# Small fills dealt evenly among the projection pieces, and conversions queued behind the last mixer's own work

## What is computed

```python
h = rms_norm(x, g1) @ W_in                        # columns split among A, B, C, D
qa, ka, va, qb, kb, vb, qc, kc, vc, qd, kd, vd = split(h)
oa = stick_breaking(qa, cache+ka, cache+va)        # scan over keys
oc = rms_norm((softmax(s0) - lam * softmax(s1)) @ vc)   # two halves per head
od = softmax(band(qd @ kd) + rel_bias) @ vd
ob = softmax_with_sink(window(qb @ kb) + t5_bias) @ vb
x = x + concat(oa, ob, oc, od) @ W_out
x = x + (silu(rms_norm(x) @ W_gate) * (rms_norm(x) @ W_up)) @ W_down
```

## Time and profile before

| | us |
|---|---|
| median of 3 runs | 1555.75 (1548.22 to 1557.88) |
| the profiled execution's own time | 1557.51 |
| its span | 1555.7 |
| rounds of A, C, D, B in the span | about 91 to 238, 238 to 444, 444 to 603, 603 to 700 |
| granted clock of TensorE, mean | 0.973 of full speed |

### The profile page before, as it was taken

One profiled execution on the slowest core, in us unless ns is written; L12 is line 12 of the kernel. 1 busy time (PEld: TensorE's weight loads), 2 busy tenths in 40 slices (PEclk: granted clock), 3 DMA queues, 4 the chain that ended last, 5 costly groups with the idle time before them and its releaser, 6 DMA issues.

```text
span 1555.7 us, 23204 instructions
## 1 busy us (share of the span) xinstructions
PE 1482.5 (95%) x8997; PEld 1307.6 (84%) x8997; DVE 691.8 (44%) x1259; ACT 417.0 (27%) x1030; POOL 270.5 (17%) x428
## 2 busy tenths in 40 slices
PE   5999999899999987999999999999999999999997
PEld 3987788687787776668899999989898999999896
DVE  6326564556533233544534444342525344443516
ACT  5123345445445545652310000101010100001013
POOL 7115454433331101122400000000000000000002
PEclk8999999799899998999999999999999999999999
DMA  7211002100011013111121111101101011110003
GB/s 210 68 62 51 15 27 66 48 15 15 15 55 47 16 32 132 42 28 41 57 80 55 41 41 54 54 27 54 54 27 54 27 54 40 42 53 27 0 0 128
DMA packets 90481, 75.93 MB, mean 49 GB/s; under 512 B 5671, under 2 KB 83016, under 8 KB 90396
## 3 DMA queue, kind: packets, MB, share of 16 engines
q1 hardware_dynamic: 90412, 75.00, 15.8%
HBM read 64.06 MB, written 10.77 MB: 48 GB/s over the span
## 4 chain that ended last, share of the span: by engine, by line
PE 87%; DVE 4%; ACT 4%; POOL 2%; issue 1%; DMA 1%; SPq 0%; ACTq 0%; DVEq 0%; POOLq 0%
PE acc L739 25%; PE acc L741 24%; PE acc L740 24%; PE acc L881 5%; PE acc L905 3%; PE acc L943 2%; PE acc L927 2%; POOL xlo L1572 1%; DVE acc L1360 1%; DVE low_z L1357 1%; PE acc L754 1%; PE acc L1049 1%; DVE wo_lo L1415 1%; DVE olo L1410 0%; PE acc L805 0%
## 5 line engine op out<-in xcount | busy, mean ns | idle before, releaser
L739 PE MATMUL acc<-ohi,gu_hi 128*128 128x384 f32 (+1 forms) x1056 | 344.3, 326 | 1.8 <-issue 1.8
L741 PE MATMUL acc<-ohi,gu_lo 128*128 128x384 f32 (+1 forms) x1056 | 344.2, 326 | 0.0
L740 PE MATMUL acc<-olo,gu_hi 128*128 128x384 f32 (+1 forms) x1056 | 344.0, 326 | 0.0
L1237 ACT ACTIVATE silu<-acc 128x384 f32<-128x384 f32 (+1 forms) x66 | 31.2, 473 | 638.6 <-PE acc L741 638.6
L739 PEld LDWEIGHTS acc<-ohi,gu_hi 128*128 128x128 f32 x1056 | 198.2, 188 | 2.7 <-issue 2.2
L740 PEld LDWEIGHTS acc<-olo,gu_hi 128*128 128x128 f32 x1056 | 198.2, 188 | 0.4
L741 PEld LDWEIGHTS acc<-ohi,gu_lo 128*128 128x128 f32 x1056 | 198.2, 188 | 0.0
L1493 DVE TENSOR_TENSOR prod<-acc,silu 128x384 f32<-128x384 f32 (+1 forms) x66 | 35.4, 536 | 336.7 <-ACT silu L1237 336.7
L1513 DVE TENSOR_TENSOR x<-acc,x 128x512 f32<-128x512 f32 x198 | 134.5, 689 | 69.1 <-PE acc L741 64.4
L1563 POOL TENSOR_SCALAR meansq<-sumsq 128x1 f32<-128x1 f32 (+1 forms) x27 | 9.2, 342 | 803.7 <-ACT sq_junk L1077 769.1
L741 PE MATMUL acc<-dn_hi,h_lo 128*128 128x512 f32 x352 | 137.1, 389 | 0.0
(11 more groups left out here) (202 smaller groups left out, 2512.1 us busy)
## 6 DMA issues: line engine op xcount, KB each, us to landing
win_raw<-in_w_in_dram SPq DMA_DIRECT2D x22, 512.0 KB, 3.9
gu_raw<-in_w_gate_dram SPq DMA_DIRECT2D x22, 512.0 KB, 3.9
gu_raw<-in_w_up_dram SPq DMA_DIRECT2D x22, 512.0 KB, 4.8
down_raw<-in_w_down_dram SPq DMA_DIRECT2D x22, 512.0 KB, 3.8
x_in<-in_x_prompt_dram SPq DMA_DIRECT2D x8, 512.0 KB, 7.0
wo_raw<-in_w_out_dram SPq DMA_DIRECT2D x8, 512.0 KB, 3.5
x<-in_x_prompt_dram SPq DMA_DIRECT2D x8, 512.0 KB, 5.2
out_dram<-y_out SPq DMA_DIRECT2D x8, 512.0 KB, 2.6
```

Source lines behind the costliest of these rows:

```text
L739: pe.matmul(out, a_hi, b_hi, start=first, stop=False)
L740: pe.matmul(out, a_hi, b_lo, start=False, stop=False)
L741: return pe.matmul(out, a_lo, b_hi, start=False, stop=last)
L1237: act.activation(silu[:, q % 2, 0:n], bank(2 * (q % 2), n), ACT.Silu).then_inc(silu_done, 1)
```

## The change

Two parts. **(1)** `mixed` loses its `every` and deals the small fills evenly over the whole list of big ones; and the cache fills, and the last rows fills of C and D, are dealt among the projection pieces of the next mixer and no longer stand as a run between the values and the projections. By the planner's own arithmetic on the new lists, no work is added or taken away (106 fills in both); what a round holds changes, in the planner's cost units (about microseconds of TensorE):

| rounds | before | after |
|---|---|---|
| 2 to 7 (A) | 6.2, 4.8, 1.4, 6.2, 0.5, 0.5 | 3.4, 6.2, 3.4, 6.2, 4.7, 4.2 |
| 8 to 15 (A) | 8.8, 7.7, 5.1, 5.6, 4.2, 2.1, 6.5, 4.2 | 5.6, 2.1, 6.4, 3.8, 2.1, 6.8, 3.8, 2.1 |
| 30 to 34 (C) | 0.5, 0.5, 4.7, 0, 4.2 | 0.5, 2.1, 2.1, 2.1, 2.1 |
| 44 to 46 (C) | 4.2, 0.9, 3.5 | 2.1, 2.7, 1.8 |
| 59 to 62 (D) | 1.4, 0.5, 8.8, 3.5 | 3.5, 4.2, 2.1, 6.1 |
| 63 to 71 (D) | 7.1, 5.6, 5.1, 7.7, 3.2, 3.7, 3.7, 2.1, 3.2 | 2.1, 8.2, 9.2, 6.0, 3.2, 3.7, 2.1, 3.2, 2.1 |

Rounds 18 to 29 and 54 to 58 keep what they had, and B's rounds have no fills. In round 69 both halves of the value fill at place 1 are gone; a rows fill at place 0 and a value fill at place 2 remain. The last pieces that use W_in slabs 19, 20 and 21, from which the rounds of W_out's conversions are counted, stay in rounds 64, 66 and 71.

**(2)** Each conversion keeps its round, and moves from the head of the round to its end: in ScalarE's queue behind `normalize`, in VectorE's behind everything but the adds of the output projection. A wait for the fourth `olo` goes before a memset in round 74.

```diff
-    def mixed(big, small, every):
-
-        small = list(small)
+    def mixed(big, small):
+
+        big, small = list(big), list(small)
+        done = 0
         for k, f in enumerate(big):
             yield f
-            if k % every == every - 1 and small:
-                yield small.pop(0)
-        yield from small
+            while done < len(small) and (done + 1) * (len(big) + 1) <= (k + 1) * (len(small) + 1):
+                yield small[done]
+                done += 1
+        yield from small[done:]
...
-    stand([*mixed(values("A", range(1, NT)), rows("A", *pairs_of_tiles), 2), *cached("A"),
-           *mixed(project("C"), biases("C"), 4), *values("C", [0])], "A")
-    stand([*mixed(values("C", range(1, NT)), rows("C", *pairs_of_tiles), 2), *cached("C"),
-           *mixed(project("D"), biases("D"), 4), *values("D", [0])], "C")
-    stand([*mixed(values("D", range(1, NT)), rows("D", *pairs_of_tiles[2:]), 3), *cached("D"),
-           *mixed(project("B"), biases("B"), 3), *mixed(values("B", range(NT)), [*cached("B"), *rows("B", (7,), (8,))], 2)], "D")
+    stand([*mixed(values("A", range(1, NT)), rows("A", *pairs_of_tiles)),
+           *mixed(project("C"), [*cached("A"), *biases("C")]), *values("C", [0])], "A")
+    stand([*mixed(values("C", range(1, NT)), rows("C", *pairs_of_tiles[:4])),
+           *mixed(project("D"), [*rows("C", (8,)), *cached("C"), *biases("D")]), *values("D", [0])], "C")
+    stand([*mixed(values("D", range(1, NT)), rows("D", *pairs_of_tiles[2:4])),
+           *mixed(project("B"), [*rows("D", (8,)), *cached("D"), *biases("B")]),
+           *mixed(values("B", range(NT)), [*cached("B"), *rows("B", (7,), (8,))])], "D")
```

In ScalarE's queue the two loops over `O_SPLITS` and `WO_SPLITS` (L1186 to L1202) go from before `for n in fill_at(r, 0)` to behind `normalize(u)`. In VectorE's:

```diff
             for r in range(rounds + 1):
-                for at, e, c in O_SPLITS:
-                    if at == r:
-                        o_count += 1
-                        dve.wait_ge(o_hi_ready, o_count)
-                        ...
                 if r < NR and pairs[r][0].mixer != "A":
                     for job in pairs[r]:
                         maximum(job)
...
                 if r == B0 + 2:
+                    dve.wait_ge(o_split, 4)
                     dve.memset(x1[DEC:P, NT - 1], 0.0)
+                for at, e, c in O_SPLITS:
+                    if at == r:
+                        o_count += 1
+                        dve.wait_ge(o_hi_ready, o_count)
+                        ...
+                for at, e in WO_SPLITS:
+                    ...
                 for k in out_at(r):
```

More of the change, by code:

```diff
@@ L1184, in _ @@
             for r in range(rounds + 1):
+                for n in fill_at(r, 0):
+                    copy_fill(n)
+                for u in units_at(r - V_LAG):
+                    if units[u][0].mixer == "C":
+                        c_square(u)
+                if r < NR:
+                    for job in pairs[r]:
+                        probabilities(job)
+                for n in fill_at(r, 1):
+                    copy_fill(n)
+                for u in units_at(r - T_LAG):
+                    copy_probs(u)
+                for n in fill_at(r, 2):
+                    copy_fill(n)
+                for u in units_at(r):
+                    if units[u][0].mixer in "DB":
+                        normalize(u)
                 for at, e, c in O_SPLITS:
@@ L1202, in _ @@
                         act.copy(wo_hi[e][:], wo_raw[e][:]).then_inc(wo_hi_ready, 1)
[L1203 to L1219, removed]
             for j in range(NT + 1):
@@ L1440, in _ @@
                 if r == B0 + 2:
+                    dve.wait_ge(o_split, 4)
                     dve.memset(x1[DEC:P, NT - 1], 0.0)
+                for at, e, c in O_SPLITS:
+                    if at == r:
+                        o_count += 1
+                        dve.wait_ge(o_hi_ready, o_count)
+                        src, high, low = o_split_parts(e, c)
+                        dve.tensor_tensor(low, src, high.bitcast(F32), ALU.subtract).then_inc(o_split, 1)
+                for at, e in WO_SPLITS:
+                    if at == r:
+                        wo_count += 1
+                        dve.wait_ge(wo_hi_ready, wo_count)
+                        dve.tensor_tensor(wo_lo[e][:], wo_raw[e][:], wo_hi[e][:].bitcast(F32), ALU.subtract)\
+                            .then_inc(wo_split, 1)
                 for k in out_at(r):
```

## The result

The changed kernel took 1573.46 us (median of 4 runs, 1567.64 to 1581.08) against 1556.66 before: a ratio of 1.0115, 95% interval 1.009 to 1.014, so slower by about 1.15%. The forecast was 1562, within 1% of before; the time lies inside the range of 1547 to 1577, but 2 us over the 1571.3 at which "slower" begins. The profiled execution spans 1579.3 us against 1555.7 and is the longest of its runs.

What follows compares the result with a forecast made beforehand. TensorE, busy 95%, bounds the kernel; only its idle and slow time can be won. From 1557.5 us: A -2.1, C -3.0 and -15.0, D +0.8, B +1.0, +16.4, +8.0 give 1563.6, for the median 1562; range 1547 to 1577.

Steps and rivals of the forecast that it cites:

- A: Rounds 6 and 7: bigger fills cover TensorE's wait for GpSimd; gain 2.1 us.
- C: Rounds 31, 33 and 45 get more fill: gaps gain 3.0 us net, full clock 15.0 us (bounds 8 and 16.5).
- the fall that I gave four chances in ten: Round 30 in C: the clock still falls for a short stretch of 6.8 us; 1.5 us charged.
- held add: B's loop: the projection add waits behind a conversion in VectorE's queue; 14.9 + 4.3 us, net loss 16.4 us.
- Rival (b): B's loop: the add isn't held, 24.4 us of loss gone, 1538 us; chance 0.1.
- start of B: Where B begins: own chain and conversions change places, residual loads wait longer; 1 us charged (bounds -3 and +4).
- clock's price of the gaps: Half clock behind new gaps: B's loop loses 8 us (bounds 0 and 13); D loses 2.2 us.
- 1.65 falls: D's rounds 67 to 69: expected clock falls behind the conversions' gaps; loss 2.2 us.
- the 1.2 us that I gave round 62: Round 62 in D: a gap of about 1.2 us, wide scores waiting for exponentials that the conversion delays.
- rival (a): C's clock falls as often as before, so the 15.0 us gain is missing: 1577 us; chance 0.15.
- (c): B's loop is held but the clock doesn't fall for it: 1554 us, or 1550; chance 0.15.
- (d): The change does nothing measurable, fills and conversions only shift their gaps: 1556 us; chance 0.1.

Runs made afterwards that it cites:

- three kernels with another list for D: Conversions moved with the old lists; changed kernel with D's old list; changed kernel with B's value fills respaced: ratios to before 1.0214, 1.0101, 1.0094.
- second profile: The changed kernel run and profiled once more, nothing edited: 1572.3 us, ratio 1.0109 to the kernel before.
- copies mid-round: Changed kernel with ScalarE's conversion copies between the pair's exponentials and the copies of transposed probabilities: 1527.4 us, ratio 0.9819 to the kernel before.
- mid-round with the adds first, respaced: Changed kernel with ScalarE's copies mid-round, VectorE's adds ahead of the differences, and small fills respaced among B's value fills: 1522.2 us, ratio 0.9801 to before.
- value fills respaced: Changed kernel with small fills respaced so rounds 66 to 71 each have a value fill or key piece at place 1: 1570.5 us, ratio 1.0094 to before.

## Why the prediction was right or wrong

**A and C were right.** A: -2.1 said, -2.6 seen. C: -3.0 of gaps and -15.0 of clock, together -18.0; seen -16.1, of which 12.3 is busy time (196.50 to 184.23 us), the clock's share, and 3.9 idle time. The clock's share is smaller than said because the fall that I gave four chances in ten came. Its waits went to 3.0 us ("3 or 4"), no half clock came behind rounds 33 and 45, and the one that did came behind round 30 (6.84 us, "6.8").

**The held add was right, step by step.** Seven waits of 18.6 us in all against 19.2 (14.9 + 4.3); five of 2.84 to 2.97 against 2.9 and 3.05, and two of 2.1 and 2.0 against 2.2; the chain of delays 4.7 us against 4.7 (from the start of its transposes, about 638.3, to 642.98). Putting the add ahead of the difference took the whole of it away, and moving ScalarE's copy did so as well. Rival (b), an add that isn't held, is out. VectorE idled 7.15 us ahead of the difference, though the add's piece was ready at 638.4. That VectorE takes its queue strictly in order is what the Trainium skill says ("TensorE: Matmul & The Clock Gate", section "Architectural detail: the array is 16× 32×32, not 1× 128×128"); the trace agrees.

**The start of B was right:** +1.0 said, +0.5 seen, with 4.9 us of waiting for `wo_lo` where I had the gate, and piece 0 at 609.34, 14.4 us after B's first scores, as said.

**The term that failed is the clock's price of the gaps, twice.** In the loop I said "a fall in four or five of the seven gaps: loss 8 us (bounds 0 and 13)", and among the signs even "half clock once or twice among them". In both profiles of the changed kernel the clock fell at all seven. TensorE was busy 29.5 us in the six slow stretches of the loop (three are shown; the others 5.73, 5.76 and 3.40) and 3.2 in the seventh behind it; half of that is 16.4 us, above my bound. The number of falls was too small, and so was the price of one: I took 1.9 us, one piece at half clock, and the four stretches of 6.8 us cost 2.8 to 2.9 each. In the three kernels with another list for D the same gaps cost about half of that in the loop, near to what I said.

In D I said 1.65 falls, a loss of 2.2 us over the kernel before; in the first profile TensorE was busy 10.24 + 28.22 us at half clock, a price of 19.2 against 6.6 before: +12.6 instead of a net of -1.0 (2.2 lost in rounds 67 to 69, 3.2 gained in 61). In the second profile D lost 4.0 in all, where I had +0.8 with an upper bound of 6. The gaps themselves I had right, 2.4 and 4.8 in rounds 67 and 69 (seen 2.5 and 4.81); only the 1.2 us that I gave round 62 didn't come. What I had not counted is that a fall among B's value fills can last: I took each for some 7 us, and the stretches were 10.2 and 30.7 in the first profile, 6.8 and 10.2 in the second.

By stages, the second profile of the changed kernel, whose time of 1573.8 is near the median, has +30.9 in the loop and behind it where I had +24.4, +4.0 in D where I had +0.8, and 1.9 less gain in C; A, the start of B and what precedes A take back 1.4. That is the 10 us between that execution (1573.8) and my 1563.6. In the first profile D alone is 11.5 over. The forecast had both overruns among its bounds ("where B stays at half clock throughout (+5) and D takes its bound (+5)") and gave this upper end, with rival (a), 0.2. So the range held because it was wide, not because the clock was priced right.

**The rivals.** (a), C's clock falling as before, did not happen: 12.3 us came back and half clock in C went from 34.1 to 6.8 us. The time is on the slow side all the same, by the term of the forecast that I took too small at both its places. (c), the loop held at full clock, is out. (d) is out: the two parts do -1.2% and +2.1%.

What stays open: why the clock's loss differs between kernels and executions with the same gaps. The runs show that it does, not what decides it. Whether respacing B's value fills removes the last fall in D isn't shown either. And C's fall behind round 30 wasn't tried by itself: in the profiles of two kernels with the same lists for C (copies mid-round, and mid-round with the adds first, respaced) it isn't there, at the same gap of 1.23 us, so it too may come or not.

## What to carry to other kernels

The end of one round and the head of the next are the same place in an engine's queue; moving work between them delays it by a round and frees nothing. What matters is what stands between an instruction and the one that waits for it: an instruction that itself waits must not stand ahead of a short one that another engine needs (here the add that gives the PSUM bank back), unless what it waits for is done by then. So put the copy where its engine idles anyway (here 1.8% faster than before, with the new lists), and price a gap on TensorE with what the clock does behind it, not by its length.

## What the runs showed of the hardware that was not expected

In the changed kernel the five gaps of 2.84 to 2.97 us in rounds 76 to 80 each came with 3.4 to 6.8 us at 1.2 GHz, so that a round of 4.7 us of work and 2.9 us of waiting took 10.2 us, not 7.6. In the kernel with the conversions only, the same five gaps brought three falls, and the rounds without one took 7.6 to 7.7.

Once at half clock, TensorE stayed there for 20.5 us (value fills respaced) and 30.7 us (changed kernel) while it was busy 19.9 and 28.2 of them, in rounds with many products of 128 columns. Those start every 0.112 us at full clock and every 0.213 at half; with 256 columns, so twice the work, it is 0.120 at full clock. A stretch can also begin in a round without a gap above 0.7 us, as that of 20.5 us did.

One program's D took 163.2 us in one execution and 171.5 in another, with the same gaps.
